# Two attention stages: probabilities normalised ahead of their transposes, and values used as the stationary matrix in two column halves

## What is computed

```python
# layer 0: half of the width is a gated linear recurrence (HGRN2, 4 heads of 128),
# half is NSA attention (8 heads of 64, 2 key/value heads): three branches
p_c = masked_softmax(s_c, cmp_end <= t)             # compressed blocks, 15 keys
o_c = einsum('bqghn,bngd->bqghd', p_c, vc_blk)
...                                                 # o_s: selected blocks, o_w: window
o = gb[..., 0:1] * o_c + gb[..., 1:2] * o_s + gb[..., 2:3] * o_w
...
out = concatenate([a_out, b_out], axis=-1) @ w_out

# layer 1: 16 heads of 64, 2 key/value heads, window of 128, a sink per head
p = exp(s - m[..., None])
den = sum(p, axis=-1) + exp(sink - m)
o = einsum('bqghk,bkgd->bqghd', p, vb) / den[..., None]
...
out = o.reshape(B, S, H * d) @ w_out
```

## Time and profile before

| | |
|---|---|
| median of 3 runs | 1196.73 us (1196.66 to 1200.32) |
| the profiled execution's own time | 1189.23 us |
| its span | 1187.4 us |
| PE busy | 889.3 us (75%) |
| DVE busy | 331.2 us (28%) |
| ACT busy | 188.8 us (16%) |
| mean of the memory read and written | 372 GB/s |
| chain that ended last: DMA 58%, PE 34%, DVE 3% | |

### The profile page before, as it was taken

One profiled execution on the slowest core, in us unless ns is written; L12 is line 12 of the kernel. 1 busy time (PEld: TensorE's weight loads), 2 busy tenths in 40 slices (PEclk: granted clock), 3 DMA queues, 4 the chain that ended last, 5 costly groups with the idle time before them and its releaser, 6 DMA issues.

```text
span 1187.4 us, 28184 instructions
## 1 busy us (share of the span) xinstructions
PE 889.3 (75%) x12538; PEld 634.0 (53%) x12538; DVE 331.2 (28%) x987; ACT 188.8 (16%) x473; POOL 28.5 (2%) x34
## 2 busy tenths in 40 slices
PE   7999999787575757575758999787666676666655
PEld 6766767565353535453535577665545453534443
DVE  3475445132120202020204553422211121111211
ACT  4223432110000000000003442101000000000000
POOL 2130000000000000000000000000000000000000
PEclk9999999999898888798889999899988788888898
DMA  9954136999999999999999742999999999999996
GB/s 376 428 196 195 71 142 259 426 407 427 427 430 428 428 429 427 429 427 429 428 428 428 315 171 77 418 413 426 428 429 427 429 427 430 427 430 427 431 427 284
DMA packets 31869, 441.85 MB, mean 372 GB/s; under 512 B 3664, under 2 KB 3792, under 8 KB 5328
## 3 DMA queue, kind: packets, MB, share of 16 engines
q1 hardware_dynamic: 31536, 441.05, 88.3%
q10 hardware_dynamic: 288, 0.15, 0.0%
HBM read 440.14 MB, written 1.05 MB: 372 GB/s over the span
## 4 chain that ended last, share of the span: by engine, by line
DMA 58%; PE 34%; DVE 3%; issue 2%; ACT 1%; SPq 1%; DVEq 0%
DMA side<-weights 54%; PE PS L480 11%; PE PS L876 7%; DMA ring<-weights 4%; PE PS L866 3%; PE PS L611 1%; PE PS L552 1%; PE PS L517 1%; PE PS L779 1%; PE PS L490 1%; PE PS L886 1%; PE PS L528 1%; SPq L315 1%; PE PS L638 1%; PE PS L846 1%
## 5 line engine op out<-in xcount | busy, mean ns | idle before, releaser
L866 PE MATMUL PS<-ring,probT 128*32 128x128 f32 x5120 | 170.1, 291 | 76.0 <-DMA ring<-weights 70.6
L866 PEld LDWEIGHTS PS<-ring,probT 128*32 128x32 f32 x5120 | 150.7, 117 | 93.4 <-DMA ring<-weights 82.5
L866 PE MATMUL PS<-side,probT 128*32 128x128 f32 x3072 | 124.5, 327 | 83.1 <-DMA side<-weights 79.7
L866 PEld LDWEIGHTS PS<-side,probT 128*32 128x32 f32 x3072 | 107.5, 132 | 108.4 <-DMA side<-weights 100.3
L480 PE MATMUL PS<-ring,side 128*128 128x512 f32 (+1 forms) x320 | 133.8, 572 | 1.4 <-ACT side L998 1.4
L1291 DVE TENSOR_TENSOR scr<-scr,PS 128x128 f32<-128x128 f32 x64 | 18.4, 288 | 400.4 <-ACT scr L1218 400.4
L1779 DVE COPY probT<-PS 32x256 f32<-32x256 f32 x128 | 54.3, 424 | 197.5 <-PE PS L876 196.6
L876 PE MATMUL PS<-side,scr 128*32 128x256 f32 x1024 | 85.7, 489 | 31.1 <-DMA side<-weights 27.3
L480 PEld LDWEIGHTS PS<-ring,side 128*128 128x128 f32 x320 | 59.6, 190 | 63.4 <-issue 62.4
L876 PE MATMUL PS<-ring,scr 128*32 128x256 f32 x1024 | 71.2, 419 | 25.9 <-DMA ring<-weights 13.9
L1222 ACT ACTIVATE probT<-PS 32x256 f32<-32x256 f32 x128 | 47.8, 374 | 264.4 <-PE PS L876 263.6
(11 more groups left out here) (244 smaller groups left out, 697.6 us busy)
## 6 DMA issues: line engine op xcount, KB each, us to landing
ring<-weights SPq DMA_DIRECT2D x127, 2048.0 KB, 34.7
side<-weights SPq DMA_DIRECT2D x80, 2048.0 KB, 27.1
ring<-weights SPq DMA_DIRECT2D x4, 512.0 KB, 8.8
xn<-xT_in SPq DMA_DIRECT2D x2, 512.0 KB, 5.6
x<-x_in SPq DMA_DIRECT2D x2, 512.0 KB, 8.9
out<-x SPq DMA_DIRECT2D x2, 512.0 KB, 2.6
TB<-table SPq DMA_DIRECT2D x1, 909.5 KB, 16.9
SM<-small SPq DMA_DIRECT2D x1, 732.0 KB, 18.2
```

What stands on the lines that cost most here:

```text
L866: mm = pe.matmul(PS[f * CAP:(f + 1) * CAP, b, up * P:(up + 1) * P], gatherT[:, k, tok], w[:, k, f * P:(f + 1) * P], start=(k == 0), stop=( ...
```

## The change

The normalisation moves from the results to the probabilities. `scale(u)` (DVE) runs between `exps(u)` and `turn_probs(u)`, which now waits for it. Its sums come from a reduction for units of 8 heads and from the accumulator of each `Exp` for units of 4 heads; the ones column of `v1` goes. `values(u)` has the values as the stationary matrix (64 columns) and the transposed probabilities moving; two matmuls write the two halves of the PSUM partitions, one for the even heads and one for the odd. The result is the attention output already transposed. In layer 0 the compressed branch and both other branches accumulate in the same PSUM bank, and `take_outputs` copies it into `hT`. `turn_cat` is left for the recurrence's half of layer 0 alone. The output projections wait for the parts of `hT` that each matmul reads. The three programs are reordered around this: in layer 0 the recurrence's last matmuls come ahead of the second gate projection, and in layer 1 the scores of the first two units come ahead of one query projection each, and the output projections are split and laid between the units. The loads and their waits are not touched. The compressed branch's `vbd` becomes stationary (8 matmuls of 128 columns in place of 4 of 256).

```diff
             def turn_probs(u):
-                pe.wait_ge(exped, u + 1)
+                pe.wait_ge(scaled, u + 1)
...
@@ -539,18 +537,22 @@
                 mm.then_inc(prob_turned, 1)
             def values(u):
-                _, _, t, h0, n = units[u]
+
+                layer, _, t, h0, n = units[u]
                 pe.wait_ge(probT_ready, u + 1)
-
-                before = u - 1 if units[u][2] == 1 and u >= 1 and units[u - 1][2] == 1 else u
-                if before >= 1:
-                    pe.wait_ge(o_done, before)
-                for j in range(n):
-                    o = PS[:, out_bank(u, j), (j % 4) * (HD + 1):(j % 4 + 1) * (HD + 1)]
+                if layer == 1 and u >= U1 + 2:
+                    pe.wait_ge(oT_ready, 3 + u - U1 - 1)
+                elif u == 4:
+                    pe.wait_ge(oT_ready, 2)
+                pT = probT[:, u % 2, :].rearrange("p (j a c) -> p j a c", j=n, a=t + 1)
+                run = 4 if layer == 0 else n
+                for j in range(0, n, run):
+                    at = ((h0 + j) // 2 if layer == 0 else j // 2) * P
                     for a in range(t + 1):
-                        c = j * (t + 1) + a
-                        mm = pe.matmul(o, probT[:, u % 2, c * P:(c + 1) * P], v1[:, a, key_slot(u, h0 + j), :],
-                                       start=(a == 0), stop=(a == t))
+                        for half in range(2):
+                            mm = pe.matmul(PS[half * HD:(half + 1) * HD, out_bank(u), at:at + run // 2 * P],
+                                           v1[:, a, key_slot(u, h0 + j), :], pT[:, j + half:j + run:2, a, :],
+                                           start=(layer == 1 and a == 0), stop=(a == t), skip_group_check=True)
                 mm.then_inc(pv_done, 1)
...
+            def turn_cat():
+
+                pe.wait_ge(cat_ready, 1)
+                for t in range(TT):
+                    for k in range(HG_H):
+                        tr = pe.transpose(PS[:, 6 + t, k * P:(k + 1) * P], cat[:, t, k * P:(k + 1) * P], ident)
+                    tr.then_inc(cat_turned, 1)
...
             def out_projection(layer, t, half, c, iters, ks=range(KD)):
                 w = cols(landed(c + half) if layer == 0 else odd_landed(c + half, iters))
-                if half == 0:
-                    pe.wait_ge(catT_ready, 2 * (TT * layer + t + 1))
-                mm = project(w, (4 if t else 6) + half, t, 512, ks)
+                if layer == 0 and half == 1:
+                    pe.wait_ge(catT_ready[1], 1)
+                for k in ks:
+                    catT_complete(layer, t, k)
+                    mm = project(w, (4 if t else 6) + half, t, 512, [k])
                 if KD - 1 in ks:
                     mm.then_inc(chunk_done if t else out_done, 1)
...
                     mm = pe.matmul(o, scT[:, h, t, :], hv[:, t, h * P:(h + 1) * P], start=(t == 0), stop=True)
             mm.then_inc(hg_o, 1)
+            project(w, 3, 1, 512).then_inc(chunk_done, 1)
+            pe.wait_ge(pc_ready, 1)
+            for g in range(2):
+                for t in range(TT):
+                    mm = pe.transpose(PS[:, 5, (g * TT + t) * P:(g * TT + t + 1) * P],
+                                      pc32[:, t, 4 * g:4 * g + 4, :].rearrange("p h n -> p (h n)"), ident)
+            mm.then_inc(pc_turned, 1)
+            scores(2)
+            pe.wait_ge(hgate_ready, 2)
+            turn_probs(0)
+            pe.wait_ge(pcT_ready, 1)
+            for t in range(TT):
+                for g in range(2):
+                    for c in range(2):
+                        pe.matmul(PS[:, 4 + t, (2 * g + c) * P:(2 * g + c + 1) * P],
+                                  vbd[:, g, 2 * c:2 * c + 2, :].rearrange("p h d -> p (h d)"), pcT[:, g, t, :],
+                                  start=(g == 0 and c == 0), stop=False, skip_group_check=True)
+            turn_probs(1)
+            scores(3)
+            values(0)
             values(1)
+            turn_cat()
             turn_probs(2)
             scores(4)
             values(2)
             turn_probs(3)
             scores(5)
...
             values(3)
+            out_projection(0, 0, 0, 9, None)
             turn_probs(4)
...
+            out_projection(0, 0, 1, 9, None, range(KD // 2))
+            values(4)
             turn_probs(5)
...
+            out_projection(0, 0, 1, 9, None, range(KD // 2, KD))
             values(5)
...
             pe.wait_ge(q_read, 3)
             keys_read(1)
             scores(U1)
+            pe.wait_ge(head_sq, G1 + 1)
+            heads_of(wq0, G1 + 4, 512).then_inc(chunk_done, 1)
             turn_queries(G1 + 3, 2)
...
             pe.wait_ge(q_read, 4)
             scores(U1 + 1)
             turn_probs(U1)
+            pe.wait_ge(head_sq, G1 + 2)
+            heads_of(wq1, G1 + 5, 512).then_inc(chunk_done, 1)
             turn_queries(G1 + 4, 6)
             values(U1)
             pe.wait_ge(q_read, 5)
             scores(U1 + 2)
             turn_probs(U1 + 1)
+            scores(U1 + 3)
             values(U1 + 1)
+            out_projection(1, 0, 0, 3, end0, range(KD // 2))
             turn_queries(G1 + 5, 7)
...
             turn_probs(U1 + 2)
             pe.wait_ge(q_read, 6)
             scores(U1 + 4)
+            out_projection(1, 0, 0, 3, end0, range(KD // 2, KD))
+            turn_probs(U1 + 3)
             values(U1 + 2)
...
             scores(U1 + 5)
             values(U1 + 3)
+            out_projection(1, 0, 1, 3, end0, range(KD // 2))
             turn_probs(U1 + 4)
...
+            out_projection(1, 0, 1, 3, end0, (4, 5))
+            values(U1 + 4)
             turn_probs(U1 + 5)
...
+            out_projection(1, 0, 1, 3, end0, (6, 7))
             values(U1 + 5)
...
                     pr = prob[:, b, j * w:(j + 1) * w]
-                    ins = act.activation(pr, pr, ACT.Exp, bias=s("nm")[:, 8 * b + j:8 * b + j + 1], scale=HD ** -0.5)
+                    c = 8 * b + j
+                    if n == 8:
+                        ins = act.activation(pr, pr, ACT.Exp, bias=s("nm")[:, c:c + 1], scale=HD ** -0.5)
+                    else:
+                        ins = act.activation(pr, pr, ACT.Exp, bias=s("nm")[:, c:c + 1], scale=HD ** -0.5,
+                                             accum_out=s("rc")[:, c:c + 1])
                 ins.then_inc(exped, 1)
...
             exps(1)
+            act.wait_ge(hg_o, 1)
+            act.activation(osq, banks(6, 2), ACT.Square).then_inc(hg_sq, 1)
+            act.wait_ge(hg_ssq, 1)
+            rsqrt(s("gr"), s("gs"), hg_rs)
             act.preload_act_table(ACT.Silu)
             act.wait_ge(hgate_done, 1)
             act.activation(hgate[:, 0, :], PS[:, 4, :], ACT.Silu).then_inc(hgate_ready, 1)
...
+            def scale(u):
                 layer, br, t, h0, n = units[u]
                 b = u % 2
+                dve.wait_ge(exped, u + 1)
+                rc = s("rc")[:, 8 * b:8 * b + n]
+                pr = prob[:, b, :].rearrange("p (h c) -> p h c", h=n)
+                if n == 8:
+                    link(dve.tensor_reduce(rc, pr, AX.X, ALU.add))
+                if layer == 1:
+                    link(tt(rc, rc, s("es")[:, 8 * (u % 4):8 * (u % 4) + n], ALU.add))
+                link(dve.reciprocal(rc, rc))
+                if layer == 0:
+                    link(tt(rc, rc, gate[:, t, h0:h0 + n, br + 1], ALU.mult))
+                if n == 8:
+                    ins = tt(pr, pr, last(rc, width(u)), ALU.mult)
+                else:
+                    for h in range(n):
+                        ins = dve.tensor_scalar(pr[:, h, :], pr[:, h, :], rc[:, h:h + 1], None, ALU.mult)
+                ins.then_inc(scaled, 1)
+
+            def take_outputs(u, c0, c1):
+
+                t = units[u][2]
+                k0 = 4 if units[u][0] == 0 else 0
+                at = 0 if units[u][0] == 0 else c0
                 dve.wait_ge(pv_done, u + 1)
...
+                dve.tensor_copy(hT[:, k0 + c0:k0 + c1, t * P:(t + 1) * P],
+                                PS[:, out_bank(u), (c0 - at) * P:(c1 - at) * P].rearrange(
+                                    "p (k t) -> p k t", k=c1 - c0)).then_inc(oT_ready, 1)
...
+            scale(0)
+            dve.wait_ge(cmp_exp, 1)
+            dve.wait_ge(zeroed, 9)
+            pcs = pc32[:, :, :, 0:16].rearrange("p a h n -> p (a h) n")
+            for t in range(TT):
+                ins = tt(pc32[:, t, :, 0:16], pc[:, t, :, :], mid(tb("cmul")[:, t * 16:(t + 1) * 16], NH), ALU.mult)
+            ins.then_inc(cmp_masked, 1)
+            dve.wait_ge(cmp_masked, 1)
+            link(dve.tensor_reduce(s("cd"), pcs, AX.X, ALU.add))
+            link(dve.tensor_scalar(s("cd"), s("cd"), 1e-30, None, ALU.max))
+            link(dve.reciprocal(s("cd"), s("cd")))
+            link(tt(s("cd").rearrange("p (a h) -> p a h", a=TT), s("cd").rearrange("p (a h) -> p a h", a=TT),
+                    gate[:, :, :, 0], ALU.mult))
```

(100 more changed lines are left out.)

148 lines of the change are left out of this document (35 added, 113 removed).

## The result

The first comparison gave 1185.72 us (median of 4 runs, 1181.67 to 1187.5) against 1196.7 us (4 runs, 1194.86 to 1200.32): ratio 0.9927, interval 0.9901 to 0.9953. The two medians lie 11.0 us apart; by the ratio, to which the interval belongs, it is 8.7 us less. The same kernel compared twice more gave 0.9913 [0.9882, 0.9944] and 0.9921 [0.9893, 0.9949]. So it is faster by 0.7 to 0.9%.

The account below looks back on a forecast made before the run. PE's way to each layer's tile-1 output projection was taken to bound the start of later loads, then memory. Layer 0 -5.7 and layer 1 -5.3 us, together -11.0, took 1196.7 to 1185.7 us; range 1181.5 to 1192.5.

Parts of the forecast that it names:

- the switching: PE at `values`: going into and out of the two-at-a-time form costs 0.1 us a side, making a unit 1.1 us.
- The values: PE, `values` in both attention stages: halves run two at a time, 0.65 us less a unit, 3.9 us less each layer.
- a sum without any drain: Whole path: with no TensorE drain at changes of tiling mode, the sum would be 12.6 us in place of 11.0.
- The serial halves: Rival, PE at `values`: halves run one after the other, a unit stays at about 1.75 us, time 1192.3 us; chance 0.1.
- The transposes of the results: PE, `turn_cat`: gone in layer 1, 16 to 8 in layer 0; 0.9 us off layer 0, 1.75 off layer 1.
- The stalls: PE's waits: layer 0, 1.6 us in the layout become 0.8; layer 1, 4.1 become 4.5.
- the layout: Orders of three engines laid out step by step, 0.05 us a hand-over; only differences between old and new were used.
- The normalisation: `scale` on DVE hidden behind PE's work; rival: PE waits at layer 1's `turn_probs`, 1206 us at 2.5 more; chance 0.04.
- The gain arrives: After the projections: loads start sooner as PE's way shortens; rival: waited out in the experts, 1196.7 us, chance 0.05.
- The loads and the tail: SP's next loads after tile 1's projections come at 177 and 719.5 us; router and choice of experts untouched.

Follow-up runs that it names:

- one_half: The changed kernel with the `values` matmuls of both halves all written to the lower 64 PSUM partitions; a single execution of 1200.07 us.
- tail_delay: The changed kernel with 16 idle matmuls ahead of tile 1's output projection in each layer; 1212.92 us, ratio 1.0153 to the kernel before.

## Why the prediction was right, and where it was off

The mechanism was right, and the median forecast was met (1185.7 against 1185.72). That it was met so closely is luck: the path shortened by 9.84 us, not 11.0, and the three comparisons give 8.7 to 10.4 by their ratios and 11.0 to 12.5 by their medians. Summing the steps of the PE timelines from start to start, stalls apart, for both kernels:

| us | layer 0: before, after | layer 1: before, after | change | forecast |
|---|---|---|---|---|
| `values`, six units | 10.56, 6.15 | 10.78, 6.14 | -9.05 | -7.8 with the switching |
| transposes of `cat` | 1.80, 0.93 | 1.75, 0 | -2.62 | -2.65 |
| all other steps | 58.82, 58.99 | 76.46, 77.03 | +0.74 | -0.1 |
| stalls | 2.03, 1.98 | 4.52, 5.66 | +1.09 | -0.4 |
| stage | 73.21, 68.05 | 93.51, 88.83 | -9.84 | -11.0 |

- **The values: right.** The records start in pairs, and a unit is 1.01 us. The rest that I had put on it as switching shows in its neighbours: the steps beside `values` grew (an 8-record projection behind it is 705.39 + 1.02 to 709.95, 3.54 us, in place of 3.43). Together -8.3, a little more than forecast. The Trainium skill, TensorEngine Tiling (Array Packing), Key Properties, says that a change of tiling mode drains TensorE: the 0.74 us over twelve units agree in kind; no run here separates the drain from other small costs. The 12.6 us that I gave for a sum without any drain doesn't follow from my own terms: 0.1 a side over twelve units is 2.4 us, which makes 13.4.
- **The serial halves: excluded, and underpriced.** 1.01 against 1.87 us of one_half decides it. The rival's time was too good, though: I had 1192.3 with units of 1.75 us, where my own bound for a unit with nothing beside it was 1.83. One_half's units take 1.87, and its stages without the slow clock give 1.5 us less than before, some 1195. The Trainium skill, TensorE: Matmul & The Clock Gate, The mechanism, has a weight load overlap matmuls in flight only when the row groups differ. Read for this case, that rule would have led to one_half's time; for two column halves with the same 128 rows this case shows the opposite.
- **The transposes of the results: right** to 0.03 us.
- **The stalls: the term that was mis-sized.** The prediction took "PE's stalls of 0.47, 0.20 and 0.63 (1.6 in the layout) become one of 0.8" and, in layer 1, "4.1 together in the layout" against 4.5. The rows have 1.30 to 1.25 us in layer 0 and 0.68 + 1.11 + 0.72 + 0.32 + 0.24 = 3.07 to 4.22 in layer 1 (0.73 and 1.45 more stand in both kernels). So the layout made the old order's stalls too long by 1.3 us in all, and a difference of layouts carried that into the sum as a gain. Each new stall by itself was near: 1.72, 1.41, 0.40 and 0.69 against 1.8, 1.5 and smaller ones. In layer 0 `values(2)` waits 1.04 us, not 0.8. The way there (the chain above) goes through two groups of exponentials and a `scale` whose multiplications take 1.14 us; I had some 0.9 for those.
- **The normalisation: hidden**, as forecast. No `turn_probs` waits for DVE. The rival's point was 1.8 us more for a unit; 1.22 us cost 6.3 us and 2.44 cost 20.6, or 16.3 at the full clock, so the gain of 9.84 is gone at about 1.5 to 1.7, a little sooner than at 1.8. The price at 2.5 us (20 us) was met with the help of the slower clock, for which it had no term; by the waits alone it was some 4 us too high.
- **The gain arrives**: tail_delay shows it one for one for time that is added, and the three comparisons agree with it for the gain.
- **The loads and the tail**: SP's loads were forecast at 177 and 719.5 us. The first came at 176.84, 5.96 us sooner than before; 5.16 of these are the change, and the rest is a sooner start of the attention in that execution. The second came at 724.57, because the experts of layer 0 took 4.7 us longer in that execution (458.90 against 454.23), not because layer 1 was slower.

## What to carry to other kernels

Where the results of two small products can go to the two halves of the PSUM partitions, put the 64-wide operand on the stationary side and let the two halves run together: the pair took the time of one here (1.01 us against 1.87), and the order in which the halves are issued didn't matter. Narrowing the stationary matrix without that gave nothing. When a layout of the steps is used for a difference, take the stalls that the trace has for the old order, not the layout's, and compare stages that repeat before comparing spans.

## What the hardware showed beyond that

- A matmul for one half of the columns starts beside earlier ones for the other half, although both use all 128 rows: 7 ns after the unit's first when it is third in the program's order, 13 ns when it is fifth.
- The accumulator's output adds 0.1 us to each exponential of 256 columns (2.08 against 1.69 us for four), although the read's own row says 0.19 us.
- Behind the same steps, the two matmuls (four records) of `keep_running` in the router's wait of layer 0 took 1.96 us in the kernel before (granted clock 1.00, the 2.4 GHz level) and 3.66 in the one after (0.50 from 190.2 to 193.6 us, the 1.2 GHz level), but 1.96 again in both other profiles of the kernel after. The last product of the last chunk took 1.97 to 3.66 us in the twelve profiles, and one and the same kernel shows both ends: 1.98 and 3.49 us before, 1.97 and 3.41 after.
- The expert stages took 453.2 to 458.9 and 457.1 to 463.3 us over twelve profiles. The level of the clock at the last products is one part of it, the landing of the last load another: 446.5 us after the router's transposes of layer 1 in the profile before, 448.7 in the second one of the same kernel. What sets that stayed open.
